# Pooling's norm and the output norm of the second attention: the mask matmuls in TensorE's waits left out

## What is computed

```python
for layer in range(DEPTH_2):
    h = rms_norm(x, mix_pre_g[layer])
    if layer < N_A:
        m = pool_mixer(h, pool_w[layer], pool_scale[layer])
    else:
        ...
        m = swa_sink_attention(q, kk, vv, sinks[j]) @ w_o[j]
    x = x + rms_norm(m, mix_post_g[layer])
    f = conv_glu_ffn(rms_norm(x, ffn_pre_g[layer]), ffn_w_in[layer], ffn_conv_w[layer],
                     ffn_conv_b[layer], ffn_w_out[layer])
    x = x + rms_norm(f, ffn_post_g[layer])
```

## Time and profile before

| | us |
|---|---|
| median of 3 runs | 854.21 |
| lowest and highest | 853.26, 854.35 |
| the profiled execution, its own time | 853.8 |
| its span, from the first to the last instruction | 852.0 |
| PE busy | 840.8 |
| DVE busy | 654.4 |
| ACT busy | 485.4 |
| mean granted TensorE clock | 1.00 |

### The profile page before, as it was taken

The page is one execution under the profiler, slowest core; times in us unless marked ns, Lnnn a source line. Parts: engine busy times, 40 slices in busy tenths (PEclk is TensorE's granted clock), DMA queues, the critical chain, the costliest instruction groups (busy, mean ns, idle before and its releaser), DMA issues.

```text
span 852.0 us, 14010 instructions
## 1 busy us (share of the span) xinstructions
PE 840.8 (99%) x5277; PEld 737.4 (87%) x5277; DVE 654.4 (77%) x869; ACT 485.4 (57%) x720; POOL 122.2 (14%) x132
## 2 busy tenths in 40 slices
PE   8999999999999999999999999999999999999997
PEld 7998989979888888879888888989876988888895
DVE  7787676777866655779788888788766878888885
ACT  6545676435444444366566656567666666566643
POOL 3192121000500000010212100000132021210100
PEclk9999999999999999999999999999999999999999
DMA  8953234556565556516555555534322455555531
GB/s 314 328 208 127 100 108 153 220 213 215 177 229 195 197 188 235 188 82 222 188 185 202 195 195 182 187 148 154 144 99 100 149 197 196 200 197 191 185 117 50
DMA packets 24085, 152.50 MB, mean 179 GB/s; under 512 B 2443, under 2 KB 3683, under 8 KB 7523
## 3 DMA queue, kind: packets, MB, share of 16 engines
q1 hardware_dynamic: 22672, 145.44, 48.1%
q10 hardware_dynamic: 1363, 6.37, 1.9%
HBM read 150.71 MB, written 1.09 MB: 178 GB/s over the span
## 4 chain that ended last, share of the span: by engine, by line
PE 74%; DVE 2%; issue 1%; ACT 1%; DVEq 0%; POOL 0%; POOLq 0%; ACTq 0%
PE ups L1174 19%; PE ups L1177 10%; PE downs L1107 7%; PE downs L1108 7%; PE downs L1109 7%; PE ups L1101 3%; PE ups L1102 3%; PE ups L1103 3%; PE ups L1221 3%; PE ups L1142 3%; PE downs L1262 1%; PE downs L1260 1%; PE ups L1113 1%; PE downs L1698 1%; PE ups L1115 1%
## 5 line engine op out<-in xcount | busy, mean ns | idle before, releaser
L1792 DVE TENSOR_TENSOR w_lo<-w,w_hi 128x2048 fp32r<-128x2048 f32 x133 | 323.2, 2435 | 63.3 <-ACT w_hi L712 60.8
L712 ACT ACTIVATE w_hi<-w 128x2048 fp32r<-128x2048 f32 x133 | 254.3, 1916 | 87.9 <-PE downs L1109 36.4
L1174 PE MATMUL ups<-x_both,w_hi 128*128 128x512 f32 x704 | 220.8, 395 | 0.0
L1177 PEld LDWEIGHTS ups<-x_both,w_lo 128*128 128x128 f32 x704 | 132.2, 188 | 31.0
L1101 PE MATMUL ups<-x_both,w_hi 128*128 128x256 f32 x480 | 138.6, 289 | 0.0
L1177 PE MATMUL ups<-x_both,w_lo 128*128 128x256 f32 x704 | 138.3, 278 | 0.0
L1102 PE MATMUL ups<-x_both,w_hi 128*128 128x256 f32 x480 | 135.7, 283 | 0.0
L1103 PE MATMUL ups<-x_both,w_lo 128*128 128x256 f32 x480 | 135.7, 283 | 0.0
L1174 PEld LDWEIGHTS ups<-x_both,w_hi 128*128 128x128 f32 x704 | 109.1, 189 | 2.0
L1107 PE MATMUL downs<-w_hi,mid 128*128 128x512 f32 x256 | 99.8, 390 | 0.0
L1108 PE MATMUL downs<-w_hi,mid 128*128 128x512 f32 x256 | 99.8, 390 | 0.0
(11 more groups left out here) (241 smaller groups left out, 1137.7 us busy)
## 6 DMA issues: line engine op xcount, KB each, us to landing
w<-w_stream SPq DMA_DIRECT2D x134, 1024.0 KB, 4.8
gates<-vec_store ACTq DMA_DIRECT2D x5, 1024.0 KB, 5.6
region<-rpb SPq DMA_DIRECT2D x2, 768.0 KB, 12.7
gates<-x_in SPq DMA_DIRECT2D x2, 512.0 KB, 3.7
result<-res SPq DMA_DIRECT2D x4, 256.0 KB, 2.0
con<-consts SPq DMA_DIRECT2D x1, 801.0 KB, 8.1
proj<-bands ACTq DMA_DIRECT2D x1, 544.0 KB, 3.9
gates<-vec_store ACTq DMA_DIRECT2D x1, 512.0 KB, 3.9
```

The source lines that it names most:

```text
L712: a.activation(hi_of(n), w32[s][:, :], ACT.Copy).then_inc(w_hi_ready, 1)
L1174: m(bank, w_hi[s][:, w], x_both[fill % 2][:, k, :, :], start=(k == 0), stop=False, skip_group_check=True)
L1177: ins = m(bank[:, T:2 * T], w_lo[s][:, w], x_hi[fill % 2][:, k, :], start=False, stop=(k == DC - 1), skip_group_check=True)
L1792: v.tensor_tensor(lo_of(n), w32[s][:, :], hi_of(n).bitcast(F32), ALU.subtract).then_inc(w_lo_ready, 1)
```

## The change

Both calls of `keep_busy` in front of `turn_first_halves` are gone, and so is the one within it, with the argument that named its bank. That is 23 matmuls fewer: six and four behind the pooling, nine and four behind the attention. Nothing else differs; what `keep_busy` wrote was read by nobody. The other calls of it stay. No other engine's program changes.

```diff
-            def turn_first_halves(k_post, fill_bank):
+            def turn_first_halves(k_post):
 
                 pe.wait_ge(x_new, new_at(k_post, 0, 0))
                 turn_half(res, 0, 0, False)
-                keep_busy(fill_bank, 4)
                 pe.wait_ge(x_part, POST.index(k_post) // 2 + 1)
                 turn_half(res, 1, 0, True, (x_new, new_at(k_post, 1, 0)))
@@
             ins = pool_part(3, 1, True)
             ins.then_inc(unit_done, 1)
-            keep_busy(aux, 6)
-            turn_first_halves(MIXPOST0, aux)
+            turn_first_halves(MIXPOST0)
@@
             for t in range(TT):
                 for q in range(2):
                     out_chunk(q, DC - 1, t)
-            keep_busy(down[2], 9)
-            turn_first_halves(MIXPOST1, wo_bank[0][0])
+            turn_first_halves(MIXPOST1)
             glu(U_GLU1, X_FFN1, FFNPRE1, MIXPOST1)
```

## The result

| | before | changed |
|---|---|---|
| median of 20 runs, us | 854.13 | 856.44 |
| lowest and highest | 853.26, 854.60 | 853.14, 858.00 |
| the profiled execution, its own time | 853.8 | 855.33 |
| its span | 852.0 | 853.5 |
| PE busy | 840.8 | 838.8 |

The ratio is 1.0024, with a 95% interval from 1.0018 to 1.0030: the changed kernel is slower, by 2.3 us between the medians and by some 2.0 us by the ratio. The spread says as much as the median. The kernel before keeps within 1.4 us; the changed one has executions as short as any of before and others almost 4 us longer. Four of its 20 lie at 853.1 to 854.0 us with a mean clock of 0.999, four at 854.9 to 855.3 with 0.997, and twelve at 856.2 to 858.0 with 0.994 to 0.996. So what the change does, it does in some executions and not in others.

A forecast was written before the change was run, and what follows sets the result against it. TensorE was taken as the bound, busy 840.8 of 852.0 us. Mask groups 0 plus clock 0 left the profiled execution at 853.8 us, so the median was forecast at 854.2, whole range 853.2 to 857.5.

The forecast's parts named there:

- the first rival: Clock falls behind the attention only, its waits being longer; price 1.6 to 3.3 us, 855.8 to 857.5 us; chance 0.26.
- Steps (1) to (4): The four mask groups, two behind the pooling, two behind the attention, fill waits that DVE ends; 0 us each.
- the weight load's releaser: DVE's sum, ending 0.05 us before the first transpose's weight load behind the pooling, taken as what ends that wait.
- the chain of waits: The profile's chain, which behind the pooling leads through six masks, 0.99 us, as if on the path.
- the bound of 0.2 us on the gain side: Most that masks still streaming when DVE is done could delay transposes: some 0.05 us a group, four groups.
- Step (5): TensorE's clock across both norms without masks: taken to hold at full level, 0 us; one fall would cost 1.6 to 3.3.
- two rows: Profile readings for no fall: 4.9 us without work after the last matmul, and the first norm's sixteen transposes with idling.
- The second rival: Clock falls behind both norms, pooling and attention; 3.2 to 6.6 us, 857.4 to 860.8 us; chance 0.15.
- The price of a fall: Slow pace at the kernel's start lasted about 3.2 us: 1.6 us lost, or twice that if waits delay recovery.
- the step of line 1221 at half pace: Sign in the feed-forward's first matmuls: steps of 0.12 us if the clock holds, 0.2 at half pace.

## Why the prediction was wrong

It forecast no change, 854.2 us; the kernel became slower by 2.3 us, to 856.44. That is within the stated range, and in time it is where the first rival was put, 855.8 to 857.5 us. That agreement is luck: the rival has one fall in every execution, behind the attention; the median comes of a mixture, with a fall behind either norm in about half of the executions when that norm's masks alone are left out.

Steps (1) to (4) held. At an unchanged clock the masks cost nothing and gave nothing: the two norms of the changed kernel have waits of 0.99, 0.63, 1.55 and 0.63 us ended by DVE's sum, and its four shortest executions, 853.1 to 854.0 us, lie where those of before do. Reading the weight load's releaser against the chain of waits was right, and doubling the masks showed the slack that this reading could not, 0.17 and 0.25 us ahead of the transposes and 0.2 us between them. That slack is why the bound of 0.2 us on the gain side was too wide. The transposes out of a longer wait took the same 0.66 us.

Step (5) failed, at its choice: it put the clock at 0, and the clock fell to 0.50 for 3.4 us behind either norm, at 1.2 to 1.6 us for a fall. It weighed two rows. The first, 4.9 us from the last matmul to the fall at full clock, was read as the idling that a fall needs. It is one sample. The same place in the other profiles shows how far it scatters: the last two matmuls of the kernel without the attention's four masks start at 845.56 and end at 846.17, and its clock falls at 848.17 (0.84 is 0.17 of the 0.25 us at 1.00), 2.0 us later:

```profile
845.56 0.61 PE L1266 MATMUL downs<-w_lo,mid 128*128 128x512 f32 x2
```

```profile
848.00:848.25 0.25, 0.00 (x0) 0.00 (x0) 0.25 (x1) 0.00 (x0) 0.00 (x0) 0.84 0.00 0
```

In the kernel with only the attention's masks left out it is 5.3 us (848.96 to 854.3). So the fall does not come at a fixed distance from the work: over the 14 profiles of this case it came 2.0 to 5.3 us behind the last matmul. With 2.0 us among them, that place of the trace gave no ground for calling 1.9 or 2.4 us of idling in a norm safe. The second row, the sixteen transposes of the first norm, was read rightly, and the run with transposes for masks agrees, as far as it goes. But it was carried too far: those 3.2 us held 1.2 us of idling and sixteen transposes, the pooling's 3.4 us hold 1.9 and eight. The prediction said itself that no stretch of the trace was as idle, and still let the two rows decide.

The second rival, both norms, was priced at 857.4 to 860.8 us, and the prediction made it the less likely because the pooling's waits are shorter. The runs show no difference: 6 of 11 executions were long with either norm's masks left out. No part of the prediction had a fall in some executions only; a single profile cannot tell such a thing, and the first one of the changed kernel alone would have pointed to the attention.

The price of a fall was put at 1.6 or 3.3 us from the pace at the kernel's start. Measured: 1.45 and 1.57 us behind the pooling, 1.2 us behind the attention, and 2.6 us where it lasted twice as long. The attention's is lower, for the part of the slow stretch that lay before the feed-forward's first matmul cost 0.07 us. The prediction also named 0.2 us as the step of line 1221 at half pace; half the pace of its 0.12 is 0.24. The loss stayed to the end, as the earlier trace rows let one expect.

## What to carry to other kernels

Where the binding engine waits and fills the wait, ask of each filler not only whether it is in the way, but what the clock does over the whole stretch, from the last dense matmul to the next; a wait may stay empty if enough is done around it, as the one of 1.55 us did with four matmuls behind it. The distance between one idle stretch and one change of the clock is no measure of how long an idle stretch is safe: look at several profiles, and compare single executions, not medians, when an effect may come in only some. Here four matmuls of 0.16 us in the middle of each stretch were enough in 11 of 11 executions, two were not in 6 of 12, and filler beyond a wait's slack of some 0.2 us cost its full 0.16 us for each matmul.

## What the runs showed of the hardware that was not expected

- Behind the pooling the clock fell with TensorE's longest wait at 0.99 us, in one profile 0.3 us after dense matmuls had begun again (385.3 us).
- Once down it stayed at 0.50 for 3.4 us, in one execution for 6.8 us, although from 661.3 us on that one had matmuls to run almost without a break.
- The same program was long in some executions and not in others: 6 of 11 with either norm's masks left out, 16 of 20 with both. One profile of it shows a fall behind the attention only, another behind both.
- In the same place of the program, behind the last matmul, the fall lagged by 2.0 to 5.3 us. Why an execution falls early or late was not tested, and stays open.
